# Neighbourhood attention: where the inverse roots of queries and keys are applied, and in which shape they are made

## What is computed

```python
def rms_norm_2(x, gain):
    y = xf * lax.rsqrt(jnp.mean(xf * xf, axis=-1, keepdims=True) + NORM_EPS)
    return (y * gain).astype(x.dtype)
...
    s_loc = einsum(q_row, k_win) * scale + bias          # 4 rows x 16 columns around the query, scale = 64 ** -0.5
    s_ctx = einsum(q_row, k_ctx) * scale
    p = softmax(concatenate([s_loc, s_ctx]))
    out = einsum(p_loc, v_win) + einsum(p_ctx, v_ctx)
```

## Time and profile before

| what | value |
|---|---|
| median of 3 runs | 1132.58 us (1132.09 to 1134.59) |
| the profiled execution | 1133.07 us, span 1131.3 us, granted clock 0.982 |
| PE busy | 1096.2 us, 97% of the span |
| PE weight loads | 999.3 us, 88% |
| DVE busy | 771.1 us, 68% |
| ACT busy | 543.8 us, 48% |
| POOL busy | 114.3 us, 10% |
| chain that ended last | PE 84%, DVE 7%, DMA 4%, ACT 2% |

### The profile page before, as it was taken

One profiled execution on the slowest core, in us unless ns is written; L12 is line 12 of the kernel. 1 busy time (PEld: TensorE's weight loads), 2 busy tenths in 40 slices (PEclk: granted clock), 3 DMA queues, 4 the chain that ended last, 5 costly groups with the idle time before them and its releaser, 6 DMA issues.

```text
span 1131.3 us, 21123 instructions
## 1 busy us (share of the span) xinstructions
PE 1096.2 (97%) x8408; PEld 999.3 (88%) x8408; DVE 771.1 (68%) x1297; ACT 543.8 (48%) x936; POOL 114.3 (10%) x131
## 2 busy tenths in 40 slices
PE   7999999999999999999999999999899999999998
PEld 2789777999999899779999999889775699999998
DVE  2498785688887678756777765748428757666665
ACT  3552475544344475555444445423137746544542
POOL 1001004000000047310000001200004310000000
PEclk8999998999999999999999999999999998999999
DMA  8971373698898615365778775446323144455450
GB/s 342 405 289 54 119 254 128 258 345 328 334 344 334 249 66 216 135 254 224 272 271 288 264 264 166 143 149 207 110 75 78 42 149 149 168 186 203 156 179 38
DMA packets 68309, 232.96 MB, mean 206 GB/s; under 512 B 12112, under 2 KB 12400, under 8 KB 67856
## 3 DMA queue, kind: packets, MB, share of 16 engines
q1 hardware_dynamic: 62208, 227.27, 56.0%
q0 software_dynamic: 5888, 3.73, 1.2%
q10 hardware_dynamic: 144, 1.05, 0.3%
HBM read 230.91 MB, written 1.05 MB: 205 GB/s over the span
## 4 chain that ended last, share of the span: by engine, by line
PE 84%; DVE 7%; DMA 4%; ACT 2%; issue 2%; POOL 1%; DVEq 0%; SPq 0%; ACTq 0%; POOLq 0%
PE bank L1579 24%; PE bank L1580 23%; PE bank L1581 23%; PE bank L2048 2%; DMA bias<-rpb 2%; PE bank L1602 2%; PE bank L1631 2%; PE bank L1717 2%; DMA a_raw<-ada 1%; DVE w_lo L997 1%; PE bank L2096 1%; DVE big L1072 1%; PE bank L1739 1%; PE bank L1654 1%; PE bank L1726 1%
## 5 line engine op out<-in xcount | busy, mean ns | idle before, releaser
L1579 PE MATMUL bank<-h_hi,w_hi 128*128 128x256 f32 (+1 forms) x1568 | 463.7, 296 | 9.5 <-DVE h_lo L1080 4.8
L1580 PE MATMUL bank<-h_lo,w_hi 128*128 128x256 f32 (+1 forms) x1568 | 454.9, 290 | 0.0
L1581 PE MATMUL bank<-h_hi,w_lo 128*128 128x256 f32 (+1 forms) x1568 | 454.6, 290 | 0.0
L997 DVE TENSOR_TENSOR w_lo<-w_raw,w_hi 128x1024 fp32r<-128x1024 f32 x271 | 327.9, 1232 | 77.5 <-ACT w_hi L609 76.4
L1579 PEld LDWEIGHTS bank<-h_hi,w_hi 128*128 128x128 f32 x1568 | 302.7, 193 | 25.5 <-issue 14.3
L609 ACT CAST w_hi<-w_raw 128x1024 fp32r<-128x1024 f32 x271 | 277.3, 1046 | 65.6 <-PE bank L1581 57.8
L1580 PEld LDWEIGHTS bank<-h_lo,w_hi 128*128 128x128 f32 x1568 | 303.5, 194 | 3.5 <-issue 0.5
L1581 PEld LDWEIGHTS bank<-h_hi,w_lo 128*128 128x128 f32 x1568 | 303.1, 193 | 3.2
L1579 PE MATMUL bank<-g_hi,w_hi 128*128 128x256 f32 x544 | 153.8, 283 | 0.2 <-DVE g_lo L1211 0.2
L1580 PE MATMUL bank<-g_lo,w_hi 128*128 128x256 f32 x544 | 152.8, 281 | 0.0
L1581 PE MATMUL bank<-g_hi,w_lo 128*128 128x256 f32 x544 | 152.7, 281 | 0.0
(11 more groups left out here) (162 smaller groups left out, 1169.9 us busy)
## 6 DMA issues: line engine op xcount, KB each, us to landing
w_raw<-weights SPq DMA_DIRECT2D x281, 512.0 KB, 4.6
a_raw<-ada SPq DMA_DIRECT2D x144, 512.0 KB, 5.2
bias<-rpb POOLq DMA_DIRECT2D x16, 224.0 KB, 7.4
xT<-xt SPq DMA_DIRECT2D x1, 1024.0 KB, 8.9
big<-ctx SPq DMA_DIRECT2D x1, 1024.0 KB, 10.5
big<-ctx ACTq DMA_DIRECT2D x1, 1024.0 KB, 6.2
out_t<-xT SPq DMA_DIRECT2D x2, 512.0 KB, 2.6
con<-consts SPq DMA_DIRECT2D x1, 928.0 KB, 13.9
```

What stands on the lines that cost most here:

```text
L997: nc.vector.tensor_tensor(w_lo[:, s, :], w_raw[:, s, :], w_hi[:, s, :].bitcast(fp), SUB)\
L1579: nc.tensor.matmul(out, a_hi, b_hi, start=start, stop=False)
L1580: nc.tensor.matmul(out, a_hi, b_lo, start=False, stop=False)
L1581: return nc.tensor.matmul(out, a_lo, b_hi, start=False, stop=stop)
```

## The change

Queries are no longer scaled before the scores. Their root without the mean's factor, sqrt(sum + 64 eps), stays in `stat` and its inverse in the new `qinv`, both with queries on partitions. The exponential takes `qinv` as its scale, the bias is multiplied by the root before it is added, and the maxima are multiplied by `qinv`, two tiles at a time. The spreads of query tiles and the multiplications into `querT` go.

Keys are still scaled. The sums of their squares are now made as two rows of 512 tokens (`of_pair` as weights, the squares moving), ACT takes the root of 2 x 512, DVE inverts 2 x 512, and PE spreads it with two matmuls over 512 columns.

```diff
@@ tensors and banks @@
+        eps_n = sb("eps_n", [P, 1])
+        qinv = sb("query_inverse", [P, 2 * NA_H])
...
         nsq = work[:, 0:1024].rearrange("p (b t) -> p b t", b=2)
+        krow = work[0:2, 1024:2048].rearrange("p (b t) -> p b t", b=2)
...
             place_stat(("qk", j), 3 + 4 * (j % 2))
-            place_tile(("inv", "qk", j), 4 + j % 2, (head_ready, MLA_H + j + 1))
+            if j < 8:
+                place_tile(("inv", "qk", j), 4 + j % 2, (head_ready, MLA_H + j + 1))
@@ gpsimd @@
             nc.gpsimd.memset(eps_q[:], QK * EPS).then_inc(const_ready, 1)
+            nc.gpsimd.memset(eps_n[:], NA_D * EPS).then_inc(const_ready, 1)
@@ scalar @@
+            def key_root(i):
+
+                b = wait_tile(act, ("sum", ("qk", i)))
+                if i >= 2:
+                    act.wait_ge(*tiles["inv", "qk", i - 2][1])
+                nc.scalar.activation(krow[:, i % 2, :], b[0:2, :], ACT.Sqrt, bias=eps[0:2, :], scale=1.0 / NA_D)\
                     .then_inc(root_ready, 1)
...
-                if j:
-                    root(("qk", j - 1), NA_D)
+                if 1 <= j <= 8:
+                    key_root(j - 1)
+                elif j:
+                    root(("qk", j - 1), 1, eps_n)
...
-                        exponential("na", 16, lambda n: 1.0, n)
+                        exponential("na", 16, lambda n: qinv[:, n:n + 1], n)
...
-            attention("na", NA_H, 16, 16, lambda n: 1.0, W_OUT2, begun=2)
+            attention("na", NA_H, 16, 16, lambda n: qinv[:, n:n + 1], W_OUT2, begun=2)
@@ vector, maximum @@
                     m0 = 3 + 2 * t
-                    ins = nc.vector.tensor_tensor(
-                        b[:, T:2 * T].rearrange("p (r c) -> p r c", r=ROWS),
-                        b[:, T:2 * T].rearrange("p (r c) -> p r c", r=ROWS),
-                        bias[:, h % BIASES, :, m0 - ROWS + 1:m0 + 1][:, :, ::-1].rearrange("p c r -> p r c"), ADD)
+                    c = STATS["qk", 8][0] + n
+                    local = b[:, T:2 * T].rearrange("p (r c) -> p r c", r=ROWS)
+                    ins = nc.vector.scalar_tensor_tensor(
+                        out=local, in0=bias[:, h % BIASES, :, m0 - ROWS + 1:m0 + 1][:, :, ::-1].rearrange("p c r -> p r c"),
+                        scalar=stat[:, c:c + 1], in1=local, op0=MUL, op1=ADD)
                     step(ins)
                     if t == 1:
                         dve.sem_inc(bias_used, 1)
-                    nc.vector.tensor_reduce(nmax[:, n:n + 1], b[:, :], AX.X, ALU.max, negate=True)\
-                        .then_inc(nmax_ready, 1)
+                    step(nc.vector.tensor_reduce(nmax[:, n:n + 1], b[:, :], AX.X, ALU.max, negate=True))
+                    if n % 2:
+                        nc.vector.tensor_tensor(nmax[:, n - 1:n + 1], nmax[:, n - 1:n + 1], qinv[:, n - 1:n + 1], MUL)\
+                            .then_inc(nmax_ready, 2)
@@ vector, the loop over the projections @@
                 if j:
                     i = j - 1
-                    n = 2 * T if i < 8 else T
-                    dst = keysT[:, i, :] if i < 8 else querT[:, i - 8, :]
-                    invert(("qk", i))
-                    inv = wait_tile(dve, ("inv", "qk", i))
-                    nc.vector.scalar_tensor_tensor(out=dst, in0=dst, scalar=1.0 if i < 8 else NA_D ** -0.5,
-                                                   in1=inv[:, 0:n], op0=MUL, op1=MUL).then_inc(head_ready, 1)
+                    dve.wait_ge(root_ready, STAT_ORDER.index(("qk", i)) + 1)
+                    if i < 8:
+                        nc.vector.reciprocal(krow[:, i % 2, :], krow[:, i % 2, :]).then_inc(inv_ready, 1)
+                        inv = wait_tile(dve, ("inv", "qk", i))
+                        nc.vector.tensor_tensor(keysT[:, i, :], keysT[:, i, :], inv[:, :], MUL).then_inc(head_ready, 1)
+                    else:
+                        c0, c1 = STATS["qk", i]
+                        nc.vector.reciprocal(qinv[:, 4 * (i - 8):4 * (i - 7)], stat[:, c0:c1]).then_inc(inv_ready, 1)
@@ tensor @@
-            def spread_qk(i):
+            def key_squares(i):
+
+                b = write_tile(pe, ("sum", ("qk", i)))
+                nc.tensor.matmul(b[0:2, :], cc("of_pair"), nsq[:, i % 2, :], start=True, stop=True)\
+                    .then_inc(full_of(("sum", ("qk", i))), 1)
+
+            def spread_key(i):
+
                 pe.wait_ge(inv_ready, STAT_ORDER.index(("qk", i)) + 1)
-                c0 = STATS["qk", i][0]
                 b = write_tile(pe, ("inv", "qk", i))
-                for t in range(4 if i < 8 else 2):
-                    for e in range(2):
-                        ins = nc.tensor.matmul(b[e * NA_D:(e + 1) * NA_D, t * P:(t + 1) * P],
-                                               column(c0 + 2 * t + e, NA_D), ident, start=True, stop=True)
+                for e in range(2):
+                    ins = nc.tensor.matmul(b[e * NA_D:(e + 1) * NA_D, :], ident[0:2, e:e + 1].broadcast_to([2, NA_D]),
+                                           krow[:, i % 2, :], start=True, stop=True)
                 ins.then_inc(full_of(("inv", "qk", i)), 1)
...
-                    sums(("qk", i), [[nsq[:, i % 2, t * P:(t + 1) * P]] for t in range(4 if i < 8 else 2)], cc("of_pair"))
-                if 1 < j < 16:
-                    spread_qk(j - 2)
+                    if i < 8:
+                        key_squares(i)
+                    else:
+                        sums(("qk", i), [[nsq[:, i % 2, t * P:(t + 1) * P]] for t in range(2)], cc("of_pair"))
+                if 1 < j < 10:
+                    spread_key(j - 2)
...
-                    if half == 0 and q4 == 1:
-                        spread_qk(14)
-                        spread_qk(15)
                     if half and q4 == 2:
-                        pe.wait_ge(head_ready, MLA_H + 16)
+                        pe.wait_ge(head_ready, MLA_H + 8)
+                        pe.wait_ge(unit_ready, 8 + 16)
                         scores("na", head_rows, 0)
```

More of the change, by code:

```diff
@@ L618, in warm @@
             def warm(func):
-                act.wait_ge(const_ready, 2)
+                act.wait_ge(const_ready, 3)
                 nc.scalar.activation(warmed[:], eps[:], func).then_inc(act_seq, 1)
@@ L629, in root @@
                 nc.scalar.activation(stat[:, c0:c1], b[:, 0:c1 - c0], ACT.Sqrt, bias=bias[:], scale=1.0 / width)\
+                    .then_inc(root_ready, 1)
+            def key_root(i):
[3 more added lines that the diff above has]
+                nc.scalar.activation(krow[:, i % 2, :], b[0:2, :], ACT.Sqrt, bias=eps[0:2, :], scale=1.0 / NA_D)\
                     .then_inc(root_ready, 1)
```

## The result

The changed kernel takes **1150.64 us** (median of 4 runs, 1149.32 to 1152.21) against 1133.59 us of the kernel before on the same chip (4 runs, 1132.09 to 1135.01). The ratio is 1.0151, with a 95% interval of 1.0128 to 1.0175. The prediction was 1137.5 us, at most 1142. The sign was right, the size was not: 17 us instead of 5.

A forecast was written before the change was run, and what follows sets the result against it. PE, busy 97% of the span, was taken as the bound, with DVE mattering where PE waits for it. The terms +10.6 - 5.3 - 1.4 - 1.9 + 3 = +5.0 us on 1132.58 gave about 1137.5 us, its own range 1133 to 1142.

The forecast's parts named there:

- Part 1: Key tiles, sums and spread on PE: fewer, wider matmuls leave PE's turn at 7.48 us, within 0.25 either way.
- Rival 4: Key turns: fewer matmuls save PE at most 0.25 us a turn; counted inside rival 1, no chance of its own.
- Part 2: Keys' reciprocal on DVE: 3.3 us over 2 x 512, turns of 8.16 us, eighth key spread 10.6 us late.
- rival 1: Keys' reciprocal: cheap per element, about 1.9 us, so the kernel gets faster, 1129.7 us; chance 0.27.
- Rival 3: Keys' reciprocal: dearer than the rows' line, 4.3 us for 512 columns, total 1146 us; chance 0.05.
- Part 3: Query tiles and values' projection: spreads and multiplications go, turns of 3.48 us; gains of 5.3, 1.4 and 1.9 us.
- 1.44 us for the clock: Query tiles, after the last two late key spreads: 1.44 us lost to a lower PE clock after idle time.
- Part 4: Attention: pairing, DVE's waits and the exponential's factor cost about 3 us, bounds 0 and about 6.5.
- steps of 3.9 us: Attention: the prediction is wrong if its steps reach 3.9 us; steps near 3.6 us were expected.
- Rival 2: Attention: the round trip gives way, pairing and waits cost 0.4 us a step, 6.5 us, total 1141 us; chance 0.12.

The follow-up runs named there:

- e5: Changed kernel with the keys' reciprocal over 2 x 512 replaced by a multiplication by 1.0 of the same shape; 1139.99 us, ratio 1.005.
- e2: Queries' half of the change alone, with the keys' sums, reciprocals and spreads as in the kernel before; 1138.1 us, ratio 1.0049.
- e1: Keys' half of the change alone, with queries and attention as in the kernel before; 1147.79 us, ratio 1.0123.
- e16: e4 with both tiles of a pair released behind the second reduction; 1142.49 us, ratio 1.0089.
- e4: Changed kernel without the multiplication of the maxima, ones as the exponential's factor, each tile released by itself; 1136.3 us, ratio 1.0033.
- e15: Changed kernel, multiplication still per pair, without POOL's masking of the biases of heads 4 to 15; 1142.64 us, ratio 1.0082.
- e3: Changed kernel with each tile's maximum multiplied and released by itself instead of two at a time; 1149.68 us, ratio 1.0136.
- e11: e3 with the multiplication written as one tensor by a scalar per partition, POOL's masking kept; 1144.33 us, ratio 1.0097.

## Why the prediction was wrong

**Part 1, sums and spread on PE: right within its bounds.** A turn gained nothing and lost 0.16 us (e5), where "within 0.25 either way" stood. Rival 4 is out.

**Part 2, the reciprocal: right.** 3.34 us against 3.3, turns of 8.18 against 8.16, the eighth spread 10.8 us late against 10.6. (3341 - 177) / 508 is 6.2 ns a column, so the row of 32 columns, the one that spoke for rival 1, was the exception. Rival 3 is out as well: 4.3 us was its condition. The Trainium skill (VectorE: DVE Perf Modes, walkthrough of the 8-slice pipeline) states a repeat count of 8, from which the prediction worked out an estimate of 8.3 ns a column. The measured 6.2 disagrees with it and decides.

**Part 3, the queries: right in kind.** Turns of 3.32 us against 3.48, which alone would have made the gain larger. It came out at 4.2 instead of 5.3. I had charged 1.44 us for the clock after the two late spreads, and the windows show 0.75 and then 0.58 over 15 us: the 6.75 us after the eighth spread hold a spread and nine tenths of a turn, 4.0 us at full clock, so 2.8 were lost there. e2, whose eighth spread is not late, agrees: it takes 21.99 us from there to the values' projection, after 24.98. So the gain itself was mis-sized the other way, 7.2 us where the sum had 6.7, and the clock's loss was 3.0 instead of 1.44. The values' projection gained 3.5 against 3.3. e1, where its idle time of 2.76 us is still there, shows whose gain that is.

**Part 4, the attention: wrong, 13.6 us instead of 3.** The step that failed is "In the steady state it is hidden while the round trip over two steps (exponential, copy, exponential, transpose, scores, two maxima: about 7 us by these durations) stays under 2 x 3.52." Both sides of that comparison were wrong. The round trip measures 7.42 us without the multiplication (e16) and 7.84 with it (after): the list has one copy, and the trace has a second one of 0.59 us behind the second exponential, for which PE waits. And PE's work for two steps is 6.65 us, since 3.52 was a mean over fourteen steps with their waits. Without the second copy the trip would be an estimated 6.9 us (7.42 less the 0.57 from the second exponential's end, 899.85, to the copy's, 900.42), still over 6.65.

The prediction named steps of 3.9 us as the sign of being wrong, and after has 7.84 / 2 = 3.92. A loop that is compared with a bound it misses by 1% has to be added up to a tenth, or be given the larger chance. Rival 2 was this mechanism, with 0.12, and its price, 6.5 us, was too low as well (its 1.2 + 14 x 0.4 is 6.8, which changes nothing here).

The terms that the runs give in its place go from e4 to after, 14.2 us; e4's attention is 0.5 shorter than that of before.

- Pairing, 9.3 us (e4 to e16). From the second scores to the fifth it is 3.0 (12.26 instead of 9.28), in the eleven steps from there to the last scores 4.9, behind them 1.4. The 0.77 us in two steps of the round trip make 4.2 of the 4.9. In the first 3.0 PE idles and its clock falls (0.91 in e16's first 20 us, 0.83 in after's, 1.00 in e4's). I had put 1.2 us there and no clock, though I had just charged it after the late spreads. PE's first transposes that wait, in after:

```profile
855.75 0.16 DVE L1136 TENSOR_TENSOR nmax<-nmax,query_inverse 128x2 f32<-128x2 f32 x1
...
857.40 2.36 PE L1746 MATMUL bank<-con,work 128*128 128x128 f32 x8 [2.72 <-ACT work L719]
```

  The 2.36 us hold two groups of four records, and the second waits for ACT's next copy. The lower clock shows in the scores behind them, which take 1.13 at full clock:

```profile
859.69 2.08 PE L1737 MATMUL bank<-big 64*128 64x512 f32 x4
```

- The multiplication itself, 1.4 us from e16 to e15, 1.0 of it between the second and the fifth scores. That is a net figure: e16 has POOL's masking, which holds up three of its `h_lo` instructions, and e15 has none. In a steady round trip the multiplication costs 7.84 - 7.42 = 0.42 us.
- POOL's masking, 3.5 us (e15 to after), all of it between the fifth and the last scores (46.75 instead of 43.25 us). Five multiplications are longer with it, four of them by 0.33 us and one by 1.46, and two `h_lo` by 0.8; in e15 all have their short lengths. No term of the sum had it. DVE's groups by form in after from 850 to 920 show the mean of an instruction that takes 0.16 alone, and the timeline the longest one:

```profile
L1136 DVE TENSOR_TENSOR nmax<-nmax,query_inverse 128x2 f32<-128x2 f32 x15 | 5.2, 346 | 1.6
```

```profile
898.69 1.62 DVE L1136 TENSOR_TENSOR nmax<-nmax,query_inverse 128x2 f32<-128x2 f32 x1
899.32 0.96 POOL L562 TENSOR_TENSOR bias<-bias,con 128x448 f32<-128x448 f32 x1
```

  898.69 + 1.62 = 900.31 and 899.32 + 0.96 = 900.28. I priced the multiplication at 0.16 a pair by the earlier trace rows, which come from the first attention, where no masking runs. The trace of before had the collision in the place that mattered, in an instruction of the same kind:

```profile
872.73 0.93 POOL L557 TENSOR_TENSOR bias<-bias,con 128x448 f32<-128x448 f32 x1 [0.79 <-DMA bias<-rpb]
872.90 1.05 DVE L1139 TENSOR_TENSOR h_lo<-ada_s,h_hi 128x256 fp32r<-128x256 f32 x1
```

  That L1139 takes 0.41 to 0.43 us in its seven other instances. It ends 0.29 us after POOL, where the small multiplications end with it.

**What stays open.** Why e5 keeps 3.0 us over e2 with a cheap instruction is only accounted for in part. Its eighth spread is 1.5 us late (56.03 instead of 54.49 from the first sums): 0.4 of that lies ahead of the first spread, the rest is 0.16 to 0.2 in each of seven turns. The other 1.5 lie behind it (23.44 instead of 21.99), where the granted clock is 0.85 from 770 to 780 us after waits of 0.18 and 0.50 us for DVE; that it is the clock was not tested. Four multiplications of after take 0.49 us. In each of them POOL's record begins 0.09 to 0.13 us before theirs ends; I have not explained that length.

## What to carry to other kernels

A round trip that nearly fills the time which hides it is added up from starts of the trace, every instruction in the way and the waits for semaphores included. It is compared with the bound engine's work in a stretch without idle time, not with the mean turn. A change that makes it longer than that is priced at the difference on every turn, plus the clock that PE loses at the first stall. An instruction that is added beside POOL's work is priced from a row where POOL works: with two tensor inputs in SBUF the smallest one can take the length of POOL's, and the form with one tensor input avoided it here. An operation whose time goes with the elements of a partition (here the reciprocal, 6.2 ns each) should be laid across partitions, even if fewer and wider matmuls beckon.

## What the runs showed of the hardware that I had not expected

- A multiplication of 128 x 1 with two tensor inputs in SBUF takes 0.16 us, or 1.28 beside POOL's masking (e3); with one tensor input it takes 0.21 in every instance (e11).
- POOL's record can begin after DVE's in such a pair (870.31 beside 870.00), while both end within 0.03 us. Which of the two waited is told by which is longer than alone, not by the starts.
- Two fp32 matmuls over 512 columns that spread a row over 64 partitions each are no cheaper than eight over 128 columns: with the sums, 0.16 us a turn dearer (7.64 in e5, 7.48 before).
- The clock fell a few microseconds after PE's idle time and stayed low while PE was fully busy (0.58 from 782 to 790 in after, behind idle times of 3.09 and 1.94 us).
